# Sums of squares by VectorE's tree, weight splits among the norm's rows, and the first loads in another order, in a two-layer streaming trunk

## What is computed

```
def rms_norm(x, w):
    y = x * rsqrt(mean(x * x, axis=-1) + EPS)
    return y * w

for layer in range(2):
    h = rms_norm(x, norm_w[layer, 0])
    m = hgrn2_mixer(h, ...) if layer == 0 else mla_mixer(h, ...)
    x = x + rms_norm(m, norm_w[layer, 1])
    f = conv_ffn(rms_norm(x, norm_w[layer, 2]), ...)
    x = x + rms_norm(f, norm_w[layer, 3])
```

## Time and profile before

| | |
|---|---|
| median of 3 runs | 2872.39 us (2866.55 to 2873.01) |
| the profiled execution | 2869.37 us, of which the span is 2867.6 |
| busy: PE, VectorE, ScalarE, GpSimd | 2723.7, 1797.5, 1256.2, 492.7 us |
| loads | 413.59 MB, mean 144 GB/s |
| mean granted PE clock | 0.978 of full speed |

### The profile page before, as it was taken

How to read it: one execution, slowest core, us unless ns; L and a number is a source line. 1 busy time by engine, 2 the same in 40 slices (tenths; PEclk the granted TensorE clock), 3 DMA queues, 4 the chain that set the end, 5 groups by cost and what they waited for, 6 DMA issues and landing times.

```text
span 2867.6 us, 56182 instructions
## 1 busy us (share of the span) xinstructions
PE 2723.7 (95%) x20018; PEld 2684.5 (94%) x20018; DVE 1797.5 (63%) x3031; ACT 1256.2 (44%) x2054; POOL 492.7 (17%) x856
## 2 busy tenths in 40 slices
PE   6999999987999999999998899898999999999997
PEld 6999999987999999999997788797999999999997
DVE  6777777756766644666657434447666644666655
ACT  5555555534444433444434444434444433444432
POOL 3112221102322200222102000002222200222200
PEclk9999999988999999999999899999999999999998
DMA  5334443333444555445553422233444455444553
GB/s 200 128 128 147 135 134 130 123 125 112 160 162 161 163 167 166 164 161 165 163 162 111 141 68 72 74 119 116 159 163 161 155 172 171 162 161 163 168 163 113
DMA packets 124257, 413.59 MB, mean 144 GB/s; under 512 B 14032, under 2 KB 22384, under 8 KB 124176
## 3 DMA queue, kind: packets, MB, share of 16 engines
q1 hardware_dynamic: 116064, 406.37, 44.1%
q10 hardware_dynamic: 7056, 3.21, 0.4%
q0 software_dynamic: 1056, 2.92, 0.3%
HBM read 406.97 MB, written 5.48 MB: 144 GB/s over the span
## 4 chain that ended last, share of the span: by engine, by line
PE 89%; DVE 7%; ACT 2%; issue 1%; DMA 1%; POOL 0%; SPq 0%; DVEq 0%; ACTq 0%; POOLq 0%
PE bank L221 28%; PE bank L223 27%; PE bank L222 27%; DVE X L834 1%; DVE h_lo L839 1%; PE bank L631 1%; DVE Y L830 1%; DMA raw<-in_w_hi_in 1%; PE bank L592 1%; PE bank L627 1%; PE bank L1267 0%; POOL ssx L814 0%; PE bank L601 0%; PE bank L1268 0%; DVE w_lo L215 0%
## 5 line engine op out<-in xcount | busy, mean ns | idle before, releaser
L221 PE MATMUL bank<-h_hi,w_hi 128*128 128x288 f32 (+1 forms) x4208 | 1281.9, 305 | 79.5 <-DVE h_lo L839 46.9
L222 PE MATMUL bank<-h_lo,w_hi 128*128 128x288 f32 (+1 forms) x4208 | 1259.7, 299 | 0.0
L223 PE MATMUL bank<-h_hi,w_lo 128*128 128x288 f32 (+1 forms) x4208 | 1255.7, 298 | 0.0
L208 ACT ACTIVATE w_hi<-raw 128x1024 fp32r<-128x1024 f32 (+2 forms) x786 | 807.8, 1036 | 942.8 <-PE bank L223 927.3
L215 DVE TENSOR_TENSOR w_lo<-raw,w_hi 128x1024 fp32r<-128x1024 f32 (+2 forms) x786 | 935.6, 1201 | 406.9 <-ACT w_hi L208 406.1
L221 PEld LDWEIGHTS bank<-h_hi,w_hi 128*128 128x128 f32 x4208 | 799.7, 190 | 91.0 <-issue 50.2
L222 PEld LDWEIGHTS bank<-h_lo,w_hi 128*128 128x128 f32 x4208 | 801.8, 191 | 1.9
L223 PEld LDWEIGHTS bank<-h_hi,w_lo 128*128 128x128 f32 x4208 | 803.0, 191 | 0.3
L221 PE MATMUL bank<-g_hi,w_hi 128*128 128x288 f32 x1408 | 416.8, 296 | 0.0
L222 PE MATMUL bank<-g_lo,w_hi 128*128 128x288 f32 x1408 | 415.4, 295 | 0.0
L223 PE MATMUL bank<-g_hi,w_lo 128*128 128x288 f32 x1408 | 413.9, 294 | 0.0
(11 more groups left out here) (243 smaller groups left out, 2388.2 us busy)
## 6 DMA issues: line engine op xcount, KB each, us to landing
raw<-in_w_fi SPq DMA_DIRECT2D x352, 512.0 KB, 4.0
raw<-in_w_hi_in SPq DMA_DIRECT2D x128, 512.0 KB, 4.1
raw<-in_w_fo SPq DMA_DIRECT2D x128, 512.0 KB, 3.6
raw<-in_w_fo SPq DMA_DIRECT2D x64, 384.0 KB, 3.2
raw<-in_w_ho SPq DMA_DIRECT2D x32, 512.0 KB, 4.0
raw<-in_w_mo SPq DMA_DIRECT2D x32, 512.0 KB, 4.0
raw<-in_w_down SPq DMA_DIRECT2D x18, 512.0 KB, 4.8
raw<-in_w_ukv SPq DMA_DIRECT2D x16, 512.0 KB, 3.7
```

The costliest lines, as they stand in the source:

```text
L208: act.activation(w_hi[:, ch.slot, 0:n], raw[:, ch.slot, 0:n], ACT.Copy).then_inc(hi_done, 1)
L221: pe.matmul(out, w_hi[:, ch.slot, w], rhs_hi, start=start, stop=False)
L222: pe.matmul(out, w_hi[:, ch.slot, w], rhs_lo, start=False, stop=False)
L223: return pe.matmul(out, w_lo[:, ch.slot, w], rhs_hi, start=False, stop=stop)
```

## The change

**The sum of squares.** GpSimd's part is gone. ScalarE writes square k to `Y[:, k, :]`, which is free once `X` has taken it in, and no longer waits for an add. When all 16 are there, VectorE adds them as a tree of four instructions (`square_sum`: 8, 4, 2 and 1 tiles of 288, the last into ssx). VectorE does this right after the split of chunk 7 (in stage 0, 1 and 3; in "down" ahead of its wait for 1/rms). PE's column sum moves from behind chunk 5 to behind chunk 6 and waits for the tree. The load of the latent cache, which goes into Y, waits for the tree of stage 2.

**Splits among the rows.** In stages 1 to 3 chunk 4 is split behind step 10 of the norm and chunk 5 behind step 13 (`EARLY`), on ScalarE and on VectorE; chunks 6 and 7 follow the norm as before.

**The start** (`start_act`, `start_dve`). SyncE issues chunk 0, x piece 0, chunk 1, x piece 1, chunks 2 and 3, x pieces 2 and 3, then chunk 4 and on. GpSimd holds back five constants until x piece 1 has landed and the other seven until x piece 3 has. Splits of chunks 0 and 1 come first, then steps 0 to 7, the splits of chunks 2 and 3, and steps 8 to 15; ScalarE's 16 squares follow, with the splits of chunks 4 to 7 among them. One table load instead of two.

```diff
@@ gemm_first
-                if k == 5:
-                    pe.wait_ge(x_added, KT * (s + 1))
+                if k == 6:
+                    pe.wait_ge(x_summed, SUMS * (s + 1))
                     pe.matmul(psum[STAT][:, 0:T], ones[:], ssx[:], start=True, stop=True).then_inc(n_sum, 1)
@@ norm_act
                     act.activation(H_HI[:, k, :], X[:, k, :], ACT.Copy, scale=norm_w[:, lb_, wb, k:k + 1]).then_inc(n_hi, 1)
-                    if q >= 2:
-                        act.wait_ge(x_added, q - 1)
-                    act.activation(SQ[k % 2], X[:, k, :], ACT.Square).then_inc(x_squared, 1)
+                    act.activation(Y[:, k, :], X[:, k, :], ACT.Square).then_inc(x_squared, 1)
+                    if k in EARLY[s]:
+                        split_hi(act, NORM_OF[s], 0, EARLY[s][k])
@@ new
+        EARLY = [{}, {10: 4, 13: 5}, {10: 4, 13: 5}, {10: 4, 13: 5}]
+        def square_sum(dve, s):
+            dve.wait_ge(x_squared, KT * (s + 1))
+            for n in range(SUMS):
+                half = KT >> (n + 1)
+                if n:
+                    dve.wait_ge(x_summed, SUMS * s + n)
+                out = ssx[:].unsqueeze(1) if half == 1 else Y[:, 0:half, :]
+                dve.tensor_tensor(out, Y[:, 0:half, :], Y[:, half:2 * half, :], ALU.add).then_inc(x_summed, 1)
@@ start_act
+            split_hi(act, IN, 0, 0)
+            split_hi(act, IN, 0, 1)
+            act.wait_ge(norm_w_in, 16)
+            for k in range(KT):
+                if k == KT // 2:
+                    split_hi(act, IN, 0, 2)
+                    split_hi(act, IN, 0, 3)
+                act.wait_ge(x_in[k // 4], 16)
+                act.activation(H_HI[:, k, :], X[:, k, :], ACT.Copy, scale=norm_w[:, lb_, wb, k:k + 1]).then_inc(n_hi, 1)
+            for k in range(KT):
+                if k % 4 == 2:
+                    split_hi(act, IN, 0, 4 + k // 4)
+                act.activation(Y[:, k, :], X[:, k, :], ACT.Square).then_inc(x_squared, 1)
@@ ffn_dve, first trip
+                    if stats and t == 0:
+                        square_sum(dve, {0: 1, 1: 3}[layer])
@@ sync
             for k in range(len(CHUNKS[IN])):
-                if k < 4:
-                    n = KT // 4
-                    sp.dma_start(X[:, k * n:(k + 1) * n, :], a["x"][:, k * n:(k + 1) * n, :]).then_inc(x_in[k], 16)
                 ring_load(sp, a["w_hi_in"], IN, 0, k, chunks_of(IN, 0)[k][0])
+                for piece in {0: [0], 1: [1], 3: [2, 3]}.get(k, []):
+                    cols = slice(piece * (KT // 4), (piece + 1) * (KT // 4))
+                    sp.dma_start(X[:, cols, :], a["x"][:, cols, :]).then_inc(x_in[piece], 16)
@@ gpsimd
-            for dst, src in loads:
+            pool.wait_ge(x_in[1], 16)
+            for dst, src in loads[:HGRN_CONSTS]:
+                pool.dma_start(dst, src).then_inc(hgrn_consts_in, 16)
+            pool.wait_ge(x_in[3], 16)
+            for dst, src in loads[HGRN_CONSTS:]:
                 pool.dma_start(dst, src).then_inc(consts_in, 16)
```

69 lines of the change are left out of this document (35 added, 34 removed).

## The result

| | before | after |
|---|---|---|
| median | 2871.45 us (2866.55 to 2873.01, 4 runs) | 2825.97 us (2824.68 to 2833.05, 4 runs) |
| ratio | | 0.9849, 95% interval 0.9829 to 0.987 |
| the profiled execution's span | 2867.6 us | 2831.3 us |
| mean granted PE clock | 0.978 | 0.982 |

The change makes the kernel 45 us faster, or 1.5%. The forecast was 2835 us (2824 to 2848). The profiled execution of after happened to be the slowest of its four.

The account below looks back on a forecast made before the run. PE, 95% busy, was bound by idle stretches at the start and three norms, where GpSimd's adds slowed VectorE. Gains 12 + 8.3 + 10.3 + 7.5 = 38.1, less 1 for clock, so 37 off the median: 2835 us (2824 to 2848).

Parts of the forecast that it names:

- s0: Program start, into hgrn_in: earlier chunk 1 and new work order bring chunk 8 forward, 12 us (11.1 to 12.6).
- s1: Norm into ffn_in00: faster VectorE rounds and early splits let PE go on at 40.11 instead of 48.46, 8.3 us.
- s2: Norm into down: earlier column sum, less a new wait of 1.5 us before chunk 8, gains 10.3 us.
- s3: Norm into ffn_in10: the same edit lets PE go on at 40.11 instead of 47.64, 7.5 us.
- clock behind the longer pauses: The two longer PE pauses in s1 and s3 can hold the clock low a little longer, -1 us.
- The rounds: VectorE's scaling, sum and h_lo for one chunk in a norm, predicted at 1.23 us a round.
- a formula that the prediction set beside its sum: Tree of adds: an fp32 tensor_tensor in SBUF takes (N + 151) / 0.96 ns, four adds 5.1 us.
- Late loads: Rival, start: chunk 1 still lands at 12.6 us, s0 gains 9 at most, 2839 us; chance 0.14.
- Not GpSimd's doing: Rival, norms: slow VectorE instructions have another cause and stay; s1 and s3 gain nothing, 2860 us; chance 0.04.
- squares that hold VectorE up: Rival, norms: ScalarE's squares, now written to Y, slow VectorE's instructions; slower kernel, 2910 us; chance 0.02.
- PE's clock: Rival: pauses in s0 to s3 each lead to 5 us at 0.51 clock, 1 to 2.4 each, 2841; chance 0.11.

Follow-up runs that it names:

- side_adds: Changed kernel plus 16 GpSimd adds of an unused spare tile in each of norms 1 to 3: 2848.41 us, ratio 0.9933.
- consts_at_once: Changed kernel with GpSimd's third HGRN scaling held until VectorE's pairs are ready, and the twelve start constants issued at once: 2829.55 us.
- before_hgrn_wait: Kernel before the change, with GpSimd's third HGRN scaling held until VectorE's pairs are ready: 2867.09 us, ratio 0.9995.
- side_memsets: Changed kernel plus four GpSimd memsets per square in norms 1 to 3, writing only: 2831.85 us, ratio 0.9873.
- after_again: The changed kernel run once more, unaltered, as the standard for runs beside it: 2825.58 us, ratio 0.9855.

## Why the prediction was right, and where it was off

| step | predicted | measured |
|---|---|---|
| s0 | 12.0 | 12.2 by chunk 8; 11.9 by norm 1 when the HGRN steps are alike |
| s1 | 8.3 | 8.8 by chunk 8 |
| s2 | 10.3 | 11.1 by chunk 8 |
| s3 | 7.5 | 8.1 by chunk 8 |
| clock behind the longer pauses | -1 | -1.1 |
| sum | 37 | 39 and 2 more in the MLA part; 40.7 between spans, 42.0 between medians |

s1 to s3 by chunk 8 are from the profiles of before and after (s1: 723.63 to 707.20, less the 7.6 us that norm 1 begins earlier; for s2, where PE has no pause in before, chunk 8's first matmul stands at 1593.91).

**The mechanism** is right. VectorE was slow because of GpSimd's adds (side_adds puts it back), and ScalarE's squares in Y hold nobody up. The rounds are 1.23 us. One reading was too narrow: the prediction ties a sum of 1.05 us to a start 0.09 us behind an add, but in the profile of before most of the slow sums start 0.35 us behind a longer add, and half of the h_lo are slow as well. The tree took 5.2 us against 5.3 (its bounds were 4.7 and 6.8), so the large adds did go by the large split's price per element. Alone they take 2.54, 1.36, 0.76 and 0.46 us, 5.1 together, which is also the estimate by a formula that the prediction set beside its sum. In norm 1 the tree ended at 29.4 us behind the first scaling (29.9 predicted), PE's sum stood at 29.5 (30.05), chunk 8 at 39.6 (40.1). The wait before chunk 4 is gone and the one before chunk 8 grew to 6.2 (6.5 predicted). At the start PE's first matmul came at 11.46 (11.1), the Exp at 36.55 (36.2 to 37.6), chunk 8 at 40.94 (40.4 to 41.9). Some waits were smaller than named: 0.36 us before the sum in s1 and s3 (1), 1.09 before chunk 8 in s2 (1.5) and 1.09 at the start (2 to 3). At the start two sizes cancel: chunks 0 and 1 took 8.6 us (7.9), so the sum came at 36.02 (35.2), and the pause behind it was shorter by 1 to 2 us. The half microsecond by which every norm did better is mostly one term: the chain to the tree's end was estimated 0.5 us too long (24.6 us to its start, 24.2 measured).

**The rivals.** Late loads: refuted by the first matmul at 11.46; consts_at_once shows what the constants would have cost (13.31). Not GpSimd's doing, and squares that hold VectorE up: refuted by the sums at 0.45 with, and 0.80 beside an add without any use. PE's clock: the 5 us at 0.50 behind chunk 8 are there in s1 and s3 (0.67 and 0.66 before), and behind chunk 4 nothing is at 0.50 any more, so the account closes at -1.1 in the profiles: 0.9 of s1's 8.8 us is given back by norm 2, and 0.3 of s3's by the end. The rival of four new cold stretches is refuted: s0 and s2 have none.

**The size.** The forecast, 2835, is 9 us above the median measured. Two terms hold it. The gain is 42 us with the HGRN steps alike, not 37: 1.9 us are the norms' half microseconds, 2 are the MLA part, where the clock falls behind three of the heads' seven pauses in before and behind two in after, 1.5 us each (below), and the rest is between spans and medians. The 2 us in the MLA part are not the work of anything that the change does there, and the prediction has no term for them: that is luck. And the gain was taken off 2872.39, the median of three runs, two of them on the high side; three further sets of before gave 2866.9 to 2869.4, and 2867.1 with the steps alike. The prediction had allowed 3 us for what lies between runs. It did not look into the HGRN loop, though the earlier trace rows is a cut of a table that has the row `PE bank L627 <- DVE Y L560: 1.5, 6, 0.3`, and there it was to be seen: some steps waited and some didn't. Norm 1 begins at 673.16 in the profile of before and at 669.61 in before_hgrn_wait, 3.5 us apart; for after it is 665.57 and 657.70, 7.9 apart, with 15 waits. The difference of the two, 4.3, is nearly all of the 4.6 us that the start's gain seemed to lose (the loop itself takes 489.9 us in the profile of before and 494.4 in that of after), and so the two first profiles differ by 36.3 us, close to the 37 predicted for a reason that is not in the prediction.

What stays open: which of the two engines gets through in the HGRN loop is not settled by what the change does. In the first profile of after and in side_memsets VectorE's product was slow in 14 steps, in side_adds in 13, in before in five and in after_again in three; I have no theory that says when.

## What to carry to other kernels

Look for an engine that does a small helper's job beside VectorE before you ask what that job costs: 16 small adds a norm, of 0.8 to 1.1 us, for which PE never stood waiting, held VectorE up by some 8 us, and a tree of four large adds on the busy engine itself took 5.2. When a wait is removed, go on along PE's timeline to the next one: here it was twice as long as before, and taking two splits out from behind it in the two FFN norms gave another 10 us (14 with the other two places). Take a gain off a kernel's usual time, not off one small sample, and find out first which part of it varies from run to run.
